# Attention's small products gathered: three places of a block in place of six

## What is computed

```python
def forgetting_attention(q, k, v, log_f):
    ...
        s = jnp.einsum('bhqd,bhkd->bhqk', q_blk, k).astype(jnp.float32) * scale
        s = s + f_blk[..., :, None] - cum_f[..., None, :]
        mask = k_pos[None, :] <= q_pos[:, None]
        p = jax.nn.softmax(jnp.where(mask, s, -jnp.inf), axis=-1)
        return jnp.einsum('bhqk,bhkd->bhqd', p.astype(v.dtype), v)
    ...
def stick_breaking_attention(q, k, v):
    ...
        z = jnp.einsum('bhqd,bhkd->bhqk', q_blk, k).astype(jnp.float32) * scale
        mask = k_pos[None, :] < q_pos[:, None]
        log_keep = jnp.where(mask, jax.nn.log_sigmoid(-z), 0.0)
        after = lax.cumsum(log_keep, axis=3, reverse=True) - log_keep
        w = jnp.where(mask, jnp.exp(jax.nn.log_sigmoid(z) + after), 0.0)
        return jnp.einsum('bhqk,bhkd->bhqd', w.astype(v.dtype), v)
    ...
def hybrid_layer(h, ...):
    u = rmsnorm(h, g_pre)
    p = u @ w_in
    ...
    o_fox = _merge_heads(o_fox) * jax.nn.silu(fgate)
    ...
    o_sb = _merge_heads(o_sb) * jax.nn.silu(sgate)
    ...
    mixed = jnp.concatenate([o_fox, o_sb, o_ssm, o_lru], axis=-1) @ w_out
    return h + rmsnorm(mixed, g_post)
```

## Time and profile before

| | us |
|---|---|
| median of three runs | 1542.29 |
| the profiled execution | 1542.66 |
| its span | 1540.9 |
| PE busy | 1521.5 |
| DVE busy | 925.0 |
| ACT busy | 861.6 |
| POOL busy | 90.0 |

### The profile page before, as it was taken

How to read it: one execution, slowest core, us unless ns; L and a number is a source line. 1 busy time by engine, 2 the same in 40 slices (tenths; PEclk the granted TensorE clock), 3 DMA queues, 4 the chain that set the end, 5 groups by cost and what they waited for, 6 DMA issues and landing times.

```text
span 1540.9 us, 22135 instructions
## 1 busy us (share of the span) xinstructions
PE 1521.5 (99%) x7090; PEld 1252.3 (81%) x7090; DVE 925.0 (60%) x1154; ACT 861.6 (56%) x1166; POOL 90.0 (6%) x130
## 2 busy tenths in 40 slices
PE   8999999999999999999999999999999999999996
PEld 6888887888888788888888888888888888888885
DVE  6544468798888894455554545455566444444445
ACT  6654476667766666565655445556666443444442
POOL 0000011211201110000000000000000000000000
PEclk9999999999999999999999999999999999999998
DMA  8466656665666666555655555565556866666674
GB/s 302 137 190 189 190 169 191 177 190 174 184 193 182 197 180 195 181 172 192 191 183 170 172 167 175 162 188 176 165 169 215 274 191 193 192 196 195 191 231 178
DMA packets 86105, 291.27 MB, mean 189 GB/s; under 512 B 9904, under 2 KB 13232, under 8 KB 86064
## 3 DMA queue, kind: packets, MB, share of 16 engines
q1 hardware_dynamic: 77328, 276.86, 59.8%
q10 hardware_dynamic: 8736, 13.89, 2.7%
HBM read 286.51 MB, written 4.19 MB: 189 GB/s over the span
## 4 chain that ended last, share of the span: by engine, by line
PE 97%; DVE 1%; DMA 1%; issue 0%; SPq 0%; ACT 0%; DVEq 0%
PE main L262 30%; PE main L264 30%; PE main L263 29%; PE side L405 2%; PE main L287 1%; DMA w_raw<-in_wall 1%; PE side L364 1%; PE side L319 0%; PE side L422 0%; PE side L399 0%; PE side L375 0%; DVE w_lo L858 0%; DVE br L1315 0%; PE side L471 0%; PE side L445 0%
## 5 line engine op out<-in xcount | busy, mean ns | idle before, releaser
L858 DVE TENSOR_TENSOR w_lo<-w_raw,w_hi 128x1024 fp32r<-128x1024 f32 x512 | 633.1, 1241 | 579.4 <-ACT w_hi L526 578.5
L526 ACT ACTIVATE w_hi<-w_raw 128x1024 fp32r<-128x1024 f32 x512 | 540.5, 1058 | 575.9 <-PE main L264 557.0
L262 PE MATMUL main<-w_hi,acts 128*128 128x512 f32 x2032 | 801.8, 395 | 2.6 <-DVE acts L989 2.6
L264 PE MATMUL main<-w_hi,acts 128*128 128x512 f32 x2032 | 791.8, 390 | 0.0
L263 PE MATMUL main<-w_lo,acts 128*128 128x512 f32 x2032 | 791.1, 389 | 0.0
L262 PEld LDWEIGHTS main<-w_hi,acts 128*128 128x128 f32 x2032 | 381.6, 188 | 86.6 <-issue 4.0
L264 PEld LDWEIGHTS main<-w_hi,acts 128*128 128x128 f32 x2032 | 381.4, 188 | 80.9
L263 PEld LDWEIGHTS main<-w_lo,acts 128*128 128x128 f32 x2032 | 381.8, 188 | 76.8
L1366 POOL TENSOR_TENSOR scr<-scr 128x256 f32<-128x256 f32 x32 | 32.2, 1005 | 490.5 <-ACT scr L618 490.5
L535 ACT ACTIVATE cross<-main,small 128x512 f32<-128x512 f32 x40 | 27.6, 689 | 28.8 <-PE main L264 28.8
L1117 DVE TENSOR_TENSOR_SCAN vals<-small,vals 128x256 f32<-128x256 f32 x64 | 41.4, 687 | 0.0
(11 more groups left out here) (250 smaller groups left out, 746.1 us busy)
## 6 DMA issues: line engine op xcount, KB each, us to landing
w_raw<-in_wall SPq DMA_DIRECT2D x512, 512.0 KB, 3.6
br<-in_x SPq DMA_DIRECT2D x16, 256.0 KB, 8.0
scr<-in_wglu ACTq DMA_DIRECT2D x8, 512.0 KB, 3.5
out<-br SPq DMA_DIRECT2D x7, 512.0 KB, 2.7
br<-in_gpost ACTq DMA_DIRECT2D x8, 256.0 KB, 4.2
vals<-in_x ACTq DMA_DIRECT2D x8, 256.0 KB, 4.8
scr<-in_x ACTq DMA_DIRECT2D x8, 256.0 KB, 4.5
scr<-in_bt ACTq DMA_DIRECT2D x32, 32.0 KB, 2.5
```

The lines of the kernel that those rows point to most:

```text
L262: pe.matmul(main[:, bank0 + a, :], u_h, wh, start=(k == 0), stop=False)
L264: mm = pe.matmul(main[:, bank0 + a, :], u_l, wh, start=False, stop=(k == NK - 1))
L526: act.activation(w_hi[:, c % RING, :], w_raw[:, c % RING, :], ACT.Copy).then_inc(hi_ready, 1)
L858: dve.tensor_tensor(w_lo[:, c % RING, :], w_raw[:, c % RING, :], w_hi[:, c % RING, :].bitcast(F32), ALU.subtract).then_inc(lo_ready, 1)
```

## The change

The small products are written at three chunks of a block: `FOX_AT` = (1, 6, 11) and `SB_AT` = (1, 7, 13). At the first stand the scores of the pair's first head, the values of the second head of the pair before, and `turn_rows`. At the second stand the first head's transposes and the second head's scores; at the third the first head's values and the second head's transposes. The second head's values thus come in the next block's chunk 1; those of the very last head stand at chunk 15 of block 23, which is written out behind a loop of three. `weighted_values` now waits until DVE has taken out the head before (`at_o`). DVE selects the first pair's heads ahead of its loop and the next pair's at chunk 9, and POOL's two loops become one, without the wait for `sel_ready`. DVE's and ACT's steps follow the new places.

```diff
--- before.py
+++ after.py
@@ -192,14 +192,14 @@
 
         N_CONST = 8
 
-        FOX_AT, SB_AT = (4, 9), (0, 7)
+        T_AT = 1
+        FOX_AT, SB_AT = (T_AT, 6, 11), (T_AT, 7, 13)
         LRU_AT = (1, 8)
         C_AT = CH - 1
         TURN_AT, TRIG_AT = (CH - 2, 0, 3, 6), (0, 1, 4, 7)
         V_READ = B_G1 * TT
         IN_FREE = N_IN_BLOCKS * TT
         T_GATE = B_V
-        T_AT = 1
         block = ctx.enter_context(nc.Block())
 
 
@@ -416,9 +416,11 @@
                 pe.transpose(side[:, 1, P:2 * P], at_p[:, P:2 * P], ident[:, :])
                 pe.transpose(side[:, 1, 2 * P:3 * P], at_p[:, 2 * P:3 * P], ident[:, :]).then_inc(at_tr, 1)
 
-            def weighted_values(h):
+            def weighted_values(h, first=False):
                 pe.wait_ge(at_ptd, h + 1)
                 pe.wait_ge(vs_ready, h + 1)
+                if not first:
+                    pe.wait_ge(at_o, h)
                 pe.matmul(side[:, 2, 0:T], at_v[:, 0, :], at_pt[:, 0:T], start=True, stop=False)
                 pe.matmul(side[:, 2, P:T], at_v[:, 1, :], at_pt[:, T:3 * P], start=False,
                           stop=True).then_inc(at_out, 1)
@@ -426,59 +428,77 @@
 
             pe.wait_ge(t_free, T_GATE)
 
+            def fox_scores(h, i, a):
+
+                pe.wait_ge(qs_ready, h + 1)
+                pe.wait_ge(sel_ready, i + 1)
+                pe.wait_ge(dec_dve, 4)
+                select = head_sel[0:ROWS, a:a + 1].to_broadcast([ROWS, P])
+                key = br[:, KEY0 + h, :]
+                q0, q1 = side[:, 0, 0:P], side[:, 0, P:3 * P]
+                pe.matmul(q0, at_q[:, 0:P], key[:, 0:P], start=True, stop=False)
+                pe.matmul(q0, select, dec_rows[:, 0:P], start=False, stop=False)
+                pe.matmul(q0, ident_b[:, :], causal_b[:, :], start=False, stop=True)
+                pe.matmul(q1, at_q[:, P:T], key[:, :], start=True, stop=False)
+                pe.matmul(q1, select, dec_rows[:, :], start=False, stop=False)
+                pe.matmul(side[:, 0, 2 * P:3 * P], ident_b[:, :], causal_b[:, :],
+                          start=False, stop=True).then_inc(at_scores, 1)
+
             def fox_block(i):
-                for c in range(CH):
-                    if c == T_AT and not isinstance(i, int):
-                        turn_rows(i + (B_G1 - 1), i + (T_GATE - 1))
-                    for a in range(2):
-                        h = i * 2 + a
-                        if c == FOX_AT[a]:
-                            pe.wait_ge(qs_ready, h + 1)
-                            pe.wait_ge(sel_ready, i + 1)
-                            pe.wait_ge(dec_dve, 4)
-                            select = head_sel[0:ROWS, a:a + 1].to_broadcast([ROWS, P])
-                            key = br[:, KEY0 + h, :]
-                            q0, q1 = side[:, 0, 0:P], side[:, 0, P:3 * P]
-                            pe.matmul(q0, at_q[:, 0:P], key[:, 0:P], start=True, stop=False)
-                            pe.matmul(q0, select, dec_rows[:, 0:P], start=False, stop=False)
-                            pe.matmul(q0, ident_b[:, :], causal_b[:, :], start=False, stop=True)
-                            pe.matmul(q1, at_q[:, P:T], key[:, :], start=True, stop=False)
-                            pe.matmul(q1, select, dec_rows[:, :], start=False, stop=False)
-                            pe.matmul(side[:, 0, 2 * P:3 * P], ident_b[:, :], causal_b[:, :],
-                                      start=False, stop=True).then_inc(at_scores, 1)
-                        if c == FOX_AT[a] + 4:
-                            pe.wait_ge(at_norm, i * 4 + 2 * a + 2)
-                            transposes(h)
-                        if c == FOX_AT[a] + 5:
-                            weighted_values(h)
+                h = i * 2
+                for c in range(CH):
+                    if c == FOX_AT[0]:
+                        fox_scores(h, i, 0)
+                        if not isinstance(i, int):
+                            weighted_values(h - 1)
+                            turn_rows(i + (B_G1 - 1), i + (T_GATE - 1))
+                    if c == FOX_AT[1]:
+                        pe.wait_ge(at_norm, i * 4 + 2)
+                        transposes(h)
+                        fox_scores(h + 1, i, 1)
+                    if c == FOX_AT[2]:
+                        weighted_values(h, isinstance(i, int))
+                        pe.wait_ge(at_norm, i * 4 + 4)
+                        transposes(h + 1)
                     chunk_in(i + B_G1, c)
 
             fox_block(0)
             with pe.Fori(1, B_G2 - B_G1) as i:
                 fox_block(i)
 
-
-            with pe.Fori(0, B_OUT - B_G2) as i:
-                for c in range(CH):
-                    for a in range(2):
-                        h = i * 2 + (FT + a)
-                        if c == SB_AT[a]:
-                            pe.wait_ge(qs_ready, h + 1)
-                            key = br[:, KEY0 + h, :]
-                            q0, q1 = side[:, 0, 0:P], side[:, 0, P:3 * P]
-                            pe.matmul(q0, at_q[:, 0:P], key[:, 0:P], start=True, stop=False)
-                            pe.matmul(q0, ident_b[:, :], strict_b[:, :], start=False, stop=True)
-                            pe.matmul(q1, at_q[:, P:T], key[:, :], start=True, stop=False)
-                            pe.matmul(side[:, 0, 2 * P:3 * P], ident_b[:, :], strict_b[:, :],
-                                      start=False, stop=True).then_inc(at_scores, 1)
-                        if c == SB_AT[a] + 6:
-                            pe.wait_ge(at_exp, i * 2 + (2 * FT + a + 1))
-                            transposes(h)
-                        if c == SB_AT[a] + 7:
-                            weighted_values(h)
-                    if c == T_AT:
+            def sb_scores(h):
+
+                pe.wait_ge(qs_ready, h + 1)
+                key = br[:, KEY0 + h, :]
+                q0, q1 = side[:, 0, 0:P], side[:, 0, P:3 * P]
+                pe.matmul(q0, at_q[:, 0:P], key[:, 0:P], start=True, stop=False)
+                pe.matmul(q0, ident_b[:, :], strict_b[:, :], start=False, stop=True)
+                pe.matmul(q1, at_q[:, P:T], key[:, :], start=True, stop=False)
+                pe.matmul(side[:, 0, 2 * P:3 * P], ident_b[:, :], strict_b[:, :],
+                          start=False, stop=True).then_inc(at_scores, 1)
+
+            def sb_block(i):
+                h = i * 2 + FT
+                for c in range(CH):
+                    if c == SB_AT[0]:
+                        sb_scores(h)
+                        weighted_values(h - 1)
                         turn_rows(i + (B_G2 - 1), i + (T_GATE + B_G2 - B_G1 - 1))
+                    if c == SB_AT[1]:
+                        pe.wait_ge(at_exp, i * 2 + (2 * FT + 1))
+                        transposes(h)
+                        sb_scores(h + 1)
+                    if c == SB_AT[2]:
+                        weighted_values(h)
+                        pe.wait_ge(at_exp, i * 2 + (2 * FT + 2))
+                        transposes(h + 1)
+                    if c == CH - 1 and isinstance(i, int):
+                        weighted_values(h + 1)
                     chunk_in(i + B_G2, c)
+
+            with pe.Fori(0, B_OUT - B_G2 - 1) as i:
+                sb_block(i)
+            sb_block(B_OUT - B_G2 - 1)
 
 
             def out_block(n, u):
@@ -744,14 +764,14 @@
                     high(i + B_G1, c + LEAD)
                     for a in range(2):
                         h = i * 2 + a
+                        if c == FOX_AT[a + 1]:
+                            copy_weights(h)
                         if c == FOX_AT[a] + 1:
                             act.wait_ge(at_max, h + 1)
                             act.activation(at_p[:, 0:P], side[:, 0, 0:P], ACT.Exp, bias=row_max[:, 0:1],
                                            accum_out=row_sum[:, 0:1]).then_inc(at_exp, 1)
                             act.activation(at_p[:, P:3 * P], side[:, 0, P:3 * P], ACT.Exp, bias=row_max[:, 1:2],
                                            accum_out=row_sum[:, 1:2]).then_inc(at_exp, 1)
-                        if c == FOX_AT[a] + 4:
-                            copy_weights(h)
                     if c == CH - 2:
                         act.activation(small[:, 146:147], later[:, 0:1], ACT.Silu)
                     if c == CH - 1:
@@ -786,7 +806,7 @@
                         if c == SB_AT[a] + 3:
                             act.wait_ge(sb_dve, i * 8 + 4 * a + 4)
                             act.activation(at_p, at_e, ACT.Exp).then_inc(at_exp, 1)
-                        if c == SB_AT[a] + 6:
+                        if c == SB_AT[a + 1]:
                             copy_weights(h)
                     if c == CH - 2:
                         act.activation(small[:, 146:147], later[:, 0:1], ACT.Silu)
@@ -1187,14 +1207,14 @@
 
 
 
+            def select_heads(i):
+
```

(57 more changed lines are left out.)

## The result

| | before | changed |
|---|---|---|
| median, us | 1542.45 | 1546.11 |
| executions | 15 | 15 |
| lowest to highest, us | 1541.86 to 1543.48 | 1544.63 to 1548.49 |
| profiled execution, us | 1542.66 | 1545.30 |
| its span, us | 1540.9 | 1543.5 |

The changed kernel takes 1.0024 of the time (95% interval 1.0017 to 1.0031): 3.66 us more. The median is the predicted one, 1546.1. It comes about in another way than predicted, and two things in the table say so at once: the profiled execution is only 2.64 us over that of before, and the changed kernel's executions spread over 4 us where the kernel before keeps within 1.6.

The account below looks back on a forecast made before the run. TensorE, busy 99% of the span, was taken as the bound, so terms are serial: 3.70 + 1.02 - 0.29 - 0.66 = +3.77 us, giving a median of 1546.1 us; range 1544.2 to 1547.8.

Parts of the forecast that it names:

- The sign and the place: Slower by 3.77 us net, mostly from TensorE waiting at block 16's first scores for POOL's copy of queries.
- that cover is gone: Block 16: scores moved from chunk 4 to 1 lose the three chunks (8.2 us) that hid the wait for queries.
- The first wait's size: Chunk 1 of block 16: TensorE waits for POOL's query copy, ending at 798.30 behind DVE's second weight subtraction; +3.70 us.
- first rival: Block 16: POOL's copy gets in between DVE's two weight subtractions; wait 2.56 us, net +2.63, 1544.9 us; chance 0.30.
- the row at 1153.40: Earlier POOL copy under five DVE instructions without a gap: 2.52 us, ended 0.26 after the run; pattern for block 16's copy.
- The rival of the falling clock: At the first wait, some 3.5 us of TensorE idling lowers the clock and costs 1.7 us more: 1547.8; chance 0.06.
- the reading of the last stretch: Kernel's end: clock still up 4.2 us behind TensorE's last product, so 3.5 us idle probably not enough to lower it.
- The last head's wait: Chunk 15 of block 23: the last weighted values wait for DVE's `head_out` of the head before; +1.02 us, 0.7 to 1.3.
- The fewer groups: Blocks 16 to 23: 25 groups of small products in place of 47, 0.03 us each; -0.66 us, between 0 and 1.3.
- The wait that went: Block 23: its first head's values no longer wait for `copy_weights`, standing six chunks behind the transposes; -0.29 us.
- The forecast's own case: Block 16's first wait is 3.7 us, POOL's copy ending about 798.3, plus 1.0 us in block 23; chance 0.46.

Follow-up runs that it names:

- x5: The changed kernel with DVE's multiplication ahead of the weight subtraction of block 15's last step, 1.2 us earlier: 1543.99 us, ratio 1.0010.
- x1: The changed kernel with block 16's groups alone at chunks 3, 7 and 11 in place of 1, 6 and 11: 1542.88 us, ratio 1.0003.
- x3: Changed kernel, block 16's groups at chunks 3, 7, 11 and pair's first head taken out one step earlier in blocks 20 to 23: 1541.81 us, ratio 0.9997.

## Why the prediction was right, and where it was not

**The sign and the place.** Right. TensorE waits at the first scores on POOL's L1421 behind DVE's L1195, and with that wait taken away the change is within the measurement of the kernel before. The step "that cover is gone" named the cause.

**The first wait's size.** Too large: 3.70 in the sum, 2.56 in the profile, which is the first rival's number to the hundredth. The step that failed is the choice of the row at 1153.40 as the pattern for a copy that meets the boundary between two DVE instructions. The copy here was let in at the boundary, as the POOL instruction at 248.79 had been. What sets the copies of 2.52 and 2.57 us apart was not found, and stays open. The Trainium skill's rule (page "SBUF — State Buffer", section "Who interferes with whom"), by which whoever issues first has the ports for its whole instruction, fits this copy, which ended 0.26 us behind the one L878 that it met; it does not explain those two.

**The clock.** The rival of the falling clock, at 0.06, came true in 11 of 23 executions. The step that failed is the reading of the last stretch: the clock stayed up there for 4.2 us behind TensorE's last product, and from that a wait of 3.5 us was taken to be probably harmless. An idle time of 2.3 us was enough in 11 of 23 and in 10 of 11 executions. One profile's end was no measure of it, since the end differs by execution as well: in the changed kernel's own profile,

```profile
1530.90:1533.00 2.10, 0.00 (x0) 0.00 (x0) 2.03 (x5) 0.81 (x3) 0.00 (x0) 1.00 1.01 406
1533.20:1543.50 10.30, 0.00 (x0) 0.00 (x0) 7.18 (x12) 0.00 (x0) 0.00 (x0) 0.50 0.74 293
```

it was down 2.4 us behind the last product's end (1530.81), and in the 13 profiles it fell between 2.1 and 4.6 us behind it. The price of a fall was taken as 1.7; two profiles give 1.5 and 1.6, and the medians of the two kinds of executions lie 1.8 apart.

**The last head's wait.** Right: 1.02 in the sum, 1.09 in the profile, 1.07 and 0.96 by two pairs of runs.

**The fewer groups.** -0.66 in the sum, -0.95 left over in the profile, within the bound of 1.3. 0.03 a group came from one pair of rows; the remainder is 0.043 a group. No run changed the number of groups alone, and the four kernels without the waits lie 0.6 to 1.2 us under the kernel before, all with intervals that reach 1: a gain is likely, and not shown.

**The wait that went.** The list no longer has it. Its 0.29 is read from the rows of before; no run measured it by itself.

**What the sum lacked.** First, TensorE's wait for `sel_ready`. The prediction followed the selection as something that POOL no longer waits for and did not ask when TensorE gets it. It lay under the longer wait, so it changed no number, but without the queries' wait it is 1.40 us, and it is what x5 ran into. Second, the end: behind TensorE's last product the changed kernel takes 12.7 us where the kernel before takes 12.2. 0.4 of the 0.5 came and went with the way POOL's loops are written; the rest is on DVE, whose last instruction ends 9.79 us behind TensorE's last product against 9.62 before. With this the two expectations that were missed come out: 1542.3 + 0.5 = 1542.8 against 1542.88 measured (x1), and 1541.2 + 0.5 = 1541.7 against 1541.81 (x3).

**Why the median was met.** On the profiled execution: 2.56 + 1.09 - 0.29 - 0.95 + 0.5 at the end = 2.9, against 2.6 measured; the 0.3 is the earlier start of block 16 (791.71 against 792.04), ahead of the change's stage. In about half of the executions the clock adds some 1.8, so that the median of all is the longest execution of the kind with the clock up, 1546.1, 0.8 over that kind's own median. The forecast had 1.1 us more in the first wait, and nothing for the clock and the end: errors that made each other good. The forecast's own case, one first wait of 3.7 us, did not come true; what came true is its first rival, with the clock's in half of the executions. That the median was met is luck.

## What to carry to other kernels

When work is moved earlier on the engine that bounds the kernel, list every semaphore that it waits for and find for each when its giver ends; the first that is late hides the next. An engine that is hardly busy (POOL, 6%) can still be the one waited for, because its order is set by another's queue. And where TensorE never waits, a single wait can cost more than its length, here 2.56 + 1.5 us or 1.6 times, since the clock may fall at it; a gain of 0.04 us a group needs about a hundred groups to pay for that.

## What the runs showed of the hardware

- The granted clock fell from 2.4 to 1.2 GHz at idle times of TensorE of 2.3 us (in 21 of 34 executions of two kernels, by mean clock and time) and 3.4 us (in the profiled execution; the times of the other four agree), and not once in 33 executions with 1.16 us. In the profile with 2.3 us it was down when the work began; in the one with 3.4 us it fell some 0.6 us into the work. Both have it low for a stretch of 3.3 us, most or all of it work.
- Behind TensorE's last product, with no more work, it fell after 2.1 to 4.6 us in the 13 profiles.
- Kernels that differ in how POOL's loops are written differ by some 0.4 us between DVE's last instruction and the end of the span: 2.52 to 2.56 us in four profiles, 2.90 to 2.95 in nine. What it is was not found.
- A wait that the list gives to "issue" was one for a semaphore of a small DVE instruction that had just ended: moving that instruction away removed it.
- POOL's copies that started under one of DVE's two-input instructions ended 0.25 or 0.26 us behind it (798.30 before, 796.84 after), and in the changed kernel's profile the next DVE instruction was 0.19 us longer. Two copies in block 23, where DVE has no pause, got in only at the end of DVE's run and took 2.52 and 2.57 us.
